# Two gate panels before the branch panels in the SSD and attention closings of a hybrid decoder trunk

## The reference, cut to what matters

```python
g_ssd, g_sgu, g_mla = jnp.split(jax.nn.sigmoid(p_gate), N_BRANCH, axis=-1)
merged = (g_ssd * (y_ssd @ w_br_ssd[i])
          + g_sgu * (y_sgu @ w_br_sgu[i])
          + g_mla * (y_mla @ w_br_mla[i]))
x = x + merged @ w_out[i]
```

## Time and profile before

| | |
|---|---|
| Time, median of 3 runs | 2109.98 us (2103.87 to 2110.43) |
| Profiled execution, first to last instruction (span) | 2098.5 us |
| PE busy | 1964.5 us, 94% of the span |
| DVE busy | 1533.4 us, 73% |
| ACT busy | 1264.9 us, 60% |
| Chain that ended last | PE 87%, DVE 6%, ACT 3% |

### The profile page before, as it was taken

The page is one execution under the profiler, slowest core; times in us unless marked ns, Lnnn a source line. Parts: engine busy times, 40 slices in busy tenths (PEclk is TensorE's granted clock), DMA queues, the critical chain, the costliest instruction groups (busy, mean ns, idle before and its releaser), DMA issues.

```text
span 2098.5 us, 24842 instructions
## 1 busy us (share of the span) xinstructions
PE 1964.5 (94%) x9464; PEld 1626.9 (78%) x9464; DVE 1533.4 (73%) x1915; ACT 1264.9 (60%) x1593; POOL 1.3 (0%) x10
## 2 busy tenths in 40 slices
PE   6898999889988898999759999999999999999998
PEld 6687877768878687887648888888888888888787
DVE  6677565554438667474459899899898989889897
ACT  4665464343435655554327777677777767777675
POOL 0000000000000000000000000000000000000000
PEclk9999998989998999998969999999999999999999
DMA  6343432435544433333459999899999999999891
GB/s 223 119 149 133 148 121 81 162 129 191 181 147 155 156 123 121 121 121 121 148 213 350 358 339 378 325 374 348 346 373 332 372 342 361 344 352 376 306 377 75
DMA packets 220045, 497.92 MB, mean 237 GB/s; under 512 B 8631, under 2 KB 14997, under 8 KB 219669
## 3 DMA queue, kind: packets, MB, share of 16 engines
q1 hardware_dynamic: 219924, 496.29, 66.1%
HBM read 495.22 MB, written 1.05 MB: 236 GB/s over the span
## 4 chain that ended last, share of the span: by engine, by line
PE 87%; DVE 6%; ACT 3%; issue 2%; DMA 1%; PEldq 0%; SPq 0%; POOLq 0%; DVEq 0%; POOL 0%; ACTq 0%
PE ps L830 12%; PE ps L832 12%; PE ps L831 12%; PE ps L885 7%; PE ps L886 6%; PE ps L887 6%; PE ps L821 6%; PE ps L823 6%; PE ps L822 6%; PE ps L1130 2%; PE ps L1142 1%; PE ps L801 1%; PE ps L778 1%; PE ps L930 1%; PE ps L928 1%
## 5 line engine op out<-in xcount | busy, mean ns | idle before, releaser
L1522 DVE TENSOR_TENSOR w_lo<-piece,w_hi 128x1024 fp32r<-128x1024 f32 (+1 forms) x742 | 855.4, 1214 | 103.5 <-ACT w_hi L1189 103.3
L1189 ACT ACTIVATE w_hi<-piece 128x1024 fp32r<-128x1024 f32 (+1 forms) x742 | 731.7, 1048 | 89.8 <-PE ps L823 37.8
L830 PE MATMUL ps<-w_hi,xg_hi 128*128 128x512 f32 x896 | 354.3, 395 | 7.5 <-POOLq L737 5.6
L832 PE MATMUL ps<-w_hi,xg_lo 128*128 128x512 f32 x896 | 349.6, 390 | 0.0
L1582 DVE TENSOR_TENSOR w_lo<-piece,mixer_hi 128x1024 fp32r<-128x1024 f32 (+1 forms) x192 | 229.3, 1216 | 164.7 <-ACT mixer_hi L1238 164.5
L831 PE MATMUL ps<-w_lo,xg_hi 128*128 128x512 f32 x896 | 349.2, 390 | 0.0
L1238 ACT ACTIVATE mixer_hi<-piece 128x1024 fp32r<-128x1024 f32 (+1 forms) x192 | 197.9, 1049 | 198.8 <-PE ps L887 165.6
L821 PE MATMUL ps<-w_hi,hid_hi 128*128 128x512 f32 x536 | 209.4, 391 | 1.5 <-DVE hid_lo L1557 1.5
L823 PE MATMUL ps<-w_hi,hid_lo 128*128 128x512 f32 x536 | 208.8, 390 | 0.0
L822 PE MATMUL ps<-w_lo,hid_hi 128*128 128x512 f32 x536 | 208.6, 389 | 0.0
L830 PEld LDWEIGHTS ps<-w_hi,xg_hi 128*128 128x128 f32 x896 | 168.7, 188 | 41.4 <-issue 8.0
(11 more groups left out here) (275 smaller groups left out, 2594.5 us busy)
## 6 DMA issues: line engine op xcount, KB each, us to landing
piece<-in_moe_w_gate SPq DMA_DIRECT2D x56, 2048.0 KB, 8.6
piece<-in_moe_w_up SPq DMA_DIRECT2D x56, 2048.0 KB, 8.9
piece<-in_moe_w_down SPq DMA_DIRECT2D x56, 2048.0 KB, 8.5
piece<-in_w_in SPq DMA_DIRECT2D x30, 2048.0 KB, 8.9
piece<-in_ffn_w_gate SPq DMA_DIRECT2D x5, 2048.0 KB, 7.8
piece<-in_ffn_w_up SPq DMA_DIRECT2D x5, 2048.0 KB, 8.0
piece<-in_ffn_w_down SPq DMA_DIRECT2D x5, 2048.0 KB, 7.8
piece<-in_w_br_ssd SPq DMA_DIRECT2D x4, 2048.0 KB, 8.5
```

What stands on the lines that cost most here:

```text
L830: pe.matmul(b, a_hi, hi[:, cs_], start=(kk == 0), stop=False)
L832: last = pe.matmul(b, a_lo, hi[:, cs_], start=False, stop=(kk == KD - 1))
L1189: act.activation(hi, slots[s][:, at_:at_ + n], ACT.Copy).then_inc(S["hi_made"], 1)
L1522: dve.tensor_tensor(w_lo[s][:, at_:at_ + n], slots[s][:, at_:at_ + n], hi.bitcast(F32), ALU.subtract).then_inc(S["lo_made"], 1)
```

## The change

In the closings of SSD and attention, the second gate panel is computed before branch panel 0 instead of behind it. The order of parts was gate 0, turned output, branch 0, gate 1, branch 1; it is now gate 0, turned output, gate 1, branch 0, branch 1. The loading order of the panels and the list of PSUM jobs follow. The SGU closing keeps its order.

```diff
     for b, br in enumerate(("ssd", "sgu", "mla")):
-        for n in range(2):
-            out += [(f"gate_{br}{n}", "in", C_GATE + D * b + N * n, N), (f"br_{br}{n}", br, N * n, N)]
+        gates = [(f"gate_{br}{n}", "in", C_GATE + D * b + N * n, N) for n in range(2)]
+        sums = [(f"br_{br}{n}", br, N * n, N) for n in range(2)]
+        out += [gates[0], sums[0], gates[1], sums[1]] if br == "sgu" else gates + sums
     out += [(f"out{n}", "out", N * n, N) for n in range(2)]
     return out
...
+BOTH_GATES_FIRST = (0, 1, 3, 2, 4)
+
+
 def closing(br):
-    return [x for i in range(5) for x in closing_part(br, i)]
+    return [x for i in BOTH_GATES_FIRST for x in closing_part(br, i)]
...
-                for i in range(5):
+                for i in BOTH_GATES_FIRST:
                     close_part("ssd", i, xh, lambda t: pe.wait_ge(S["y_normed"], t + 1))
...
-                for i in range(5):
+                for i in BOTH_GATES_FIRST:
                     close_part("mla", i, o, lambda t: pe.wait_ge(S["o_made"], (4, 12)[t]))
```

## The result

The changed kernel takes 2078.57 us (median of 4 runs, 2076.97 to 2090.64); the kernel before took 2109.89 on the same chip (4 runs, 2103.87 to 2110.43). The ratio is 0.9868, with a 95% interval of 0.9838 to 0.9897; it is estimated over all runs, and the quotient of the two medians alone would be 0.9852. Forecast were 2087.5 us, a gain of 22.5 us; by the interval the gain is 22 to 34 us. The medians of two further sets of runs (e1 and e9) lie inside it.

What follows compares the result with a forecast made beforehand. PE bounds the kernel, so only its idle or slow time can be gained: 18.9 us idle plus 5.8 of slow clock less 2.2 of new waits give 22.5, so 2109.98 becomes 2087.5 us; range 2079 to 2096.

Steps and rivals of the forecast that it cites:

- The wait for `yT_lo` goes, and PE starts at once: Behind the closings' transposes: gate panel 1 fills PE's idle stall, 6.8 us in SSD or 2.4 in attention.
- The sums of the closings: Savings per closing: SSD 7.5 us in layer 0, 8.5 in layer 1; attention 2.5 and 3.95.
- the distances after: From the transposes' start to branch panel 1's start: 25.1 us in SSD closings, 23.9 in attention.
- New waits of 1.1 us per SSD closing: PE waits for gate panel 1's fourth piece and branch panel 0's first, together 1.1 us per SSD closing.
- 5.8 us of slow clock: Half-clock matmuls behind the old stalls vanish: 1.64 and 2.70 us in SSD, 1.43 in layer 1's attention closing.
- stalls gone, slow clock not: Rival, chance 0.12: idle time in the closings goes but slow clock stays; gain 16.7 us, time 2093.3.
- Transfers at nothing, nothing given back: Moved panel loads cost nothing, hidden by 11.1 us of PE work against 8.9; later stages take nothing back.
- the sign that the prediction set itself: Prediction is wrong if the stretch from branch panel 1's start to the layer's end has grown; no size given.
- the first rival: The rival "stalls gone, slow clock not", chance 0.12: later stalls falling otherwise may cost as much slow clock; 2093.3 us.
- The single gate tile: Second sigmoids wait for branch 0's merge; the fourth piece of branch panel 1 keeps 3.3 us of slack.
- The rival: "Slower", chance 0.02: in the closings the gate tile delays ACT's queue and PE beyond the slack; 2117 us.

Runs made afterwards that it cites:

- e1: The changed kernel again, no edit, against the kernel before: 2085.1 us (6 runs), ratio 0.9902.
- e9: The changed kernel once more, on one chip with the kernel that splits the awaited pieces first: 2085.44 us (6 runs), ratio 0.9913 to the kernel before.
- e2: The kernel before with the new order in the SSD closings only, attention closings in the old order: 2088.8 us, ratio 0.9931.
- e3: The kernel before with the new order in the attention closings only, SSD closings in the old order: 2100.63 us, ratio 0.9976.
- e6: The changed kernel with gate panel 1's fourth piece and branch panel 0's first piece split ahead of key work on DVE: 2080.73 us, ratio 0.9886.
- e5: The changed kernel with one extra DVE reduction before the split of gate panel 1's fourth piece, each SSD closing: 2084.64 us, ratio 0.9909.
- e4: The kernel before, old order kept, with 27 extra matmuls of 512 columns put into each SSD stall: 2098.97 us, ratio 0.9972.
- e8: The changed kernel with three extra DVE reductions ahead of the merge of branch 0 in the SSD closings: 2095.06 us, ratio 0.9955.
- e7: The changed kernel with one extra DVE reduction ahead of the merge of branch 0 in the SSD closings: 2083.68 us, ratio 0.9895.

## Why the prediction was right

**The wait for `yT_lo` goes, and PE starts at once.** Right in all closings; e2 and e3 show that each half does it for its own.

**The sums of the closings.** 7.5, 8.5, 2.5 and 3.95 were forecast; 7.43, 8.52, 2.63 and 4.06 were measured. What was really forecast are the distances after, 25.1 and 23.9, and the three traces of the changed kernel agree on them to 0.12 us. The differences belong to one trace of before: with the old order as e3 and e2 ran it, they would be 7.2 and 7.2 for SSD, 4.1 and 2.6 for attention.

**New waits of 1.1 us per SSD closing.** Right as a sum: 0.40 and 0.56 by the steps, and 1.13 and 1.06 by comparison with e6. The causes are shown: e5 makes the first longer by the length of one more instruction on DVE, e6 removes both by moving the awaited splits up. The Trainium skill, "TensorE: Matmul & The Clock Gate", the table at its head, says that VectorE works its queue strictly first in, first out. The traces agree: the splits at 206.53 and 209.87 stand behind the turned output and the key scaling, and moving them in program order was enough.

**5.8 us of slow clock.** The mechanism is shown: e4 gives 4.2 us back in the SSD closings with the stall as long as ever, against the 4.3 read from the rows. No run filled the attention waits, so for their 1.43 it is carried over. The size is that of one execution: the SSD part is 4.3 in the trace of before and 2.8 in e3's, the attention part 1.43 there and 1.50 in e2's, but in the other layer. The rival "stalls gone, slow clock not" expected 16.7 us in all. The times don't rule it out, as 16.7 lies in the intervals of e1 (16 to 25) and of e9 (12 to 24); the traces do for the closings, since none of the three of the changed kernel shows slow matmuls in one.

**Transfers at nothing, nothing given back.** Right in the main: the only new waits in the closings are for `w_lo`. But the sign that the prediction set itself, a longer stretch behind the closings, did appear: two of the stretches above are 2.6 and 2.2 us longer. It isn't work given back, since PE's idle time there is 36.8 us against 36.7 and 6.6 against 7.1, and the difference is clock. The sum had no term for slow clock that moves, though the first rival names it, and the sign could not tell it from a real loss.

**The single gate tile.** 3.3 us of slack forecast, 3.6 measured (e8, and e7 inside it). The rival needed a merge some 10 us later; it is where it was worked out to be, 223.6 against 223.9.

**The total.** The first median, 2078.6, was 9 us below the forecast. No step of the sum accounts for that. The forecast was the median of before less 22.5, and both medians are samples of a scatter: the changed kernel's profiled and timed runs there had spans from 2075.0 us (granted clock 0.974) to 2088.7 (0.966), all with the same instructions. The repeats, 21.4 us (e1) and 17.4 (e9), lie on both sides with the first 31.3 around 22.5. The median of before on the first chip, 2109.89, is also 3.4 to 7.0 us above the medians of 23, 13 and 11 runs on the other chips, and the first one of the changed kernel 5.7 below the 2084.3 of all its runs; both widen the first gain. What sets how much slow clock an execution gets is not settled by these runs.

## What to carry to other kernels

Where PE waits for a producer chain on another engine, look for PE work whose inputs are already there and put it into the gap; count the slow clock behind the stall with the idle time, here 4.3 us on 13.9 in one trace and 2.8 in another. Then look at the queue of the engine that feeds the cover: the pieces for it stood behind work that nobody waited for, and moving them up was worth another 2.2 us in the trace. Add up such changes from distances between the same two instructions in both traces, since the median of four executions was 9 us off here.

## What the runs showed of the hardware

- Matmuls whose result is thrown away made a kernel faster: 27 in each of two stalls, 0.28% (e4, ratio 0.9972). They kept the granted clock of what follows at its higher level, 2.4 GHz: 1.00 over both panels, where the kernel before has 0.52 in the 3.49 us behind the stall.
- Equal waits don't have equal sequels: 2.55 us in e5 and 3.20 us in e8 were each followed by full clock in layer 0 (records of 0.50) and by half clock in layer 1 (0.79 and 0.80). The attention wait was followed by half clock in layer 1 before (2.36 us) and in layer 0 in e2 (2.36), by full clock in the other layer. The Trainium skill, "TensorE: Matmul & The Clock Gate", section "Part 1: The HAM clock gate", says that the chip samples on a beat not tied to the kernel, so that slow matmuls vary in number. These pairs agree with it.
- One kernel's executions spread over 18 us (2076.97 to 2095.01 in 16 runs), with the granted clock between 0.975 and 0.965. The 6.8 us that the closings of e5 took longer did not show in its median of four.
